# Two gates and two products of the attention's branch behind each retention head, in place of all sixteen tiles behind the last

## The reference

```python
h = rms_norm(x, g_mix[l]); z = h @ w_in[l]
qa, ka, va, ga, ub, vb, qc, kc, vc, gates = split_cols(z)
ya = retention(rotary(qa), rotary(ka), va)          # 4 heads of 128
ya = silu(ga) * rms_normalize(ya) * ret_norm_g[l]
yb = spatial_gating(gelu(ub), gelu(vb), ...)        # 4 groups of 128
yc = dilated window attention(qc, kc, vc)           # 3 groups x 4 heads, mixed by their denominators
gt = sigmoid(gates)                                 # 3 branches x 1024
merged = gt[0] * (ya @ w_branch[l, 0]) + gt[1] * (yb @ w_branch[l, 1]) + gt[2] * (yc @ w_branch[l, 2])
x = x + merged @ w_o[l]
x = x + (silu(rms_norm(x) @ gate) * (rms_norm(x) @ up)) @ w_down[l]
```

## Time and profile before

| what | value |
|---|---|
| median of 3 runs | 1910.8 us (1909.89 to 1911.27) |
| the profiled execution | 1910.71 us |
| its span, first to last instruction | 1908.9 us |
| TensorE, matmuls busy | 1894.6 us, 99% of the span |
| VectorE busy | 1246.4 us, 65% |
| ScalarE busy | 844.4 us, 44% |
| granted TensorE clock over the span | 1.000 |

### The profile page before, as it was taken

How to read it: one execution, slowest core, us unless ns; L and a number is a source line. 1 busy time by engine, 2 the same in 40 slices (tenths; PEclk the granted TensorE clock), 3 DMA queues, 4 the chain that set the end, 5 groups by cost and what they waited for, 6 DMA issues and landing times. The chain is left out here.

```text
span 1908.9 us, 26594 instructions
## 1 busy us (share of the span) xinstructions
PE 1894.6 (99%) x10632; PEld 1699.3 (89%) x10632; DVE 1246.4 (65%) x1625; ACT 844.4 (44%) x1186; POOL 96.9 (5%) x148
## 2 busy tenths in 40 slices
PE   8999999999999999999999999999999999999999
PEld 7888888888888899899888888888888888998998
DVE  7767767746566786377576667677365657863775
ACT  5544444524234464155335444345242344642554
POOL 0000001111111000000000000011111110000000
PEclk9999999999999999999999999999999999999999
DMA  5322356787777355366333222577777773653663
GB/s 203 95 78 67 89 135 182 190 221 206 205 204 207 93 177 173 100 191 198 120 100 95 67 78 83 144 199 185 210 211 211 194 201 92 193 159 107 201 210 122
DMA packets 85897, 295.68 MB, mean 155 GB/s; under 512 B 20368, under 2 KB 20624, under 8 KB 84624
## 3 DMA queue, kind: packets, MB, share of 16 engines
q1 hardware_dynamic: 73104, 218.49, 36.8%
q0 software_dynamic: 12672, 75.51, 17.1%
HBM read 291.79 MB, written 77.66 MB: 194 GB/s over the span
## 5 line engine op out<-in xcount | busy, mean ns | idle before, releaser
L1057 ACT ACTIVATE w_high<-raw 128x1024 fp32r<-128x1024 f32 x396 | 418.3, 1057 | 791.7 <-PE bank L847 663.1
L1266 DVE TENSOR_TENSOR w_low<-raw,w_high 128x1024 fp32r<-128x1024 f32 x396 | 483.0, 1222 | 147.6 <-ACT w_high L1057 141.0
L847 PE MATMUL bank<-h_high,w_high 128*128 128x512 f32 x1408 | 543.5, 386 | 8.9 <-DVE h_low L1271 8.2
L847 PE MATMUL bank<-h_low,w_high 128*128 128x512 f32 x1408 | 534.3, 379 | 0.0
L847 PE MATMUL bank<-h_high,w_low 128*128 128x512 f32 x1408 | 534.1, 379 | 0.0
L847 PEld LDWEIGHTS bank<-h_high,w_high 128*128 128x128 f32 x1408 | 266.7, 189 | 47.0 <-issue 8.1
L847 PEld LDWEIGHTS bank<-h_high,w_low 128*128 128x128 f32 x1408 | 266.6, 189 | 38.0
L847 PEld LDWEIGHTS bank<-h_low,w_high 128*128 128x128 f32 x1408 | 266.8, 189 | 36.2
L847 PE MATMUL bank<-in_high,w_high 128*128 128x512 f32 x672 | 255.0, 379 | 0.0
L847 PE MATMUL bank<-in_low,w_high 128*128 128x512 f32 x672 | 254.7, 379 | 0.0
L847 PE MATMUL bank<-in_high,w_low 128*128 128x512 f32 x672 | 254.7, 379 | 0.0
(11 more groups left out here) (163 smaller groups left out, 2344.3 us busy)
## 6 DMA issues: line engine op xcount, KB each, us to landing
raw<-weights SPq DMA_DIRECT2D x325, 512.0 KB, 4.1
weight_sums<-weights POOLq DMA_DIRECT2D x108, 512.0 KB, 6.1
raw<-weight_sums SPq DMA_DIRECT2D x72, 512.0 KB, 3.8
weight_sums<-weight_sums POOLq DMA_DIRECT2D x36, 512.0 KB, 4.1
turned<-rows SPq DMA_DIRECT2D x3, 768.0 KB, 6.8
xT<-x_t SPq DMA_DIRECT2D x8, 256.0 KB, 5.4
decay_sb<-decay SPq DMA_DIRECT2D x8, 256.0 KB, 5.0
out_t<-xT SPq DMA_DIRECT2D x8, 256.0 KB, 6.4
```

Of the source, the lines that this page charges most:

```text
L847: return pe.matmul(o, w, m, start=start, stop=stop)
L1057: act.activation(w_high[:, PART_SLOT[s], :, :], raw[:, s % RAW_SLOTS, :, :], ACT.Copy).then_inc(part_high_w.sem, 1)
L1266: dve.tensor_tensor(w_low[:, PART_SLOT[s], :, :], raw[:, s % RAW_SLOTS, :, :], w_high[:, PART_SLOT[s], :, :], ALU.subtract).then_inc(part_ ...
```

## The change

The sixteen tiles of `gated(2)` are dealt out: behind the four tiles of retention head h come gate(2, 2h), gate(2, 2h+1), proj(2, 2h), proj(2, 2h+1). The relative places of `schedule` stay as they are, so the steps t+4 to t+7 of every head now hang on these four tiles, and t+8 on rq of the next head, or on sv(0) for head 3. As `merged[7]`, the row that `ret_std` had, is now written before head 3 is through, `ret_std` moves to row 7. As sv(0) now follows the last head directly, the order of the token banks is changed so that `out_bank` comes last, and the wait for the copy out of it stands at the fourth bank's first matmul.

```diff
     for h in range(HEADS):
         t += [("k", h, g) for g in range(N_GROUP)] + [("q", h, g) for g in range(N_GROUP)]
         t += [("v", h, g) for g in range(N_GROUP)]
-    for h in range(HEADS):
-        t += [("rq", h), ("rk", h), ("rv", h), ("rg", h)]
-
-    def gated(branch):
+
+    def gated(branch, pairs=range(KT // 2)):
         out = []
-        for n in range(0, KT, 2):
+        for n in pairs:
+            n *= 2
             out += [("gate", branch, n), ("gate", branch, n + 1), ("proj", branch, n), ("proj", branch, n + 1)]
         return out
 
-    t += gated(2)
+    for h in range(HEADS):
+        t += [("rq", h), ("rk", h), ("rv", h), ("rg", h)] + gated(2, [h])
...
-        ret_std, k_std2 = work[:, 16, :], work[:, 17, :]
+        ret_std, k_std2 = work[:, 7, :], work[:, 17, :]
...
-        token_bank = score_bank + [out_bank, stat_bank]
+        token_bank = score_bank + [stat_bank, out_bank]
...
                 if j == 0:
-                    pe.wait_ge(ret_copied.sem, ret_copied.at(base, HEADS - 1))
                     pe.wait_ge(std_ready.sem, std_ready.at(base, "cq", HEADS - 1))
...
                     for b in range(BLK):
+                        if k == 0 and b == BLK - 1:
+                            pe.wait_ge(ret_copied.sem, ret_copied.at(base, HEADS - 1))
                         hi, lo = (h[:, k, b * P:(b + 1) * P] for h in (h_high, h_low))
```

## The result

| | median us | runs | lowest to highest |
|---|---|---|---|
| before | 1910.59 | 22 | 1909.73 to 1911.59 |
| changed | 1913.12 | 22 | 1912.48 to 1914.03 |

The account below looks back on a forecast made before the run. TensorE was taken as the bound in the retention heads, so only stalls could change: 3.0 - 0.2 = +2.8 us, all other terms 0, giving 1913.5 us; range 1911.0 to 1916.5.

Parts of the forecast that it names:

- (a): Two gates, two projections behind each head: heads 0 to 2 each gain head 3's 0.50 us stall, +3.0 us over two layers.
- (b): Head 3: sv(0) behind its `rowstat` waits for no evacuation, so the last 0.10 us goes: -0.2 us over two layers.
- (c): Token banks reordered, wait for the copy at the fourth bank, `ret_std` in another row: 0, bounds 0 to 0.3 us.
- (d): Seam to the next head: VectorE's rotations, evacuations and splits come right behind the reciprocal; slack 2.0 us, cost 0.
- rival of a backlog: VectorE over 2.0 us later than laid out at the seams; a half-tile slip gives 1917.1 us; chance 0.08.
- (e): Head 0: proj(2,0) reads attention head 3's low half with its tenth matmul; slack 0.42 us, cost 0.
- (f): ScalarE's function tables: 12 loads a layer in place of 10, 5.1 us more of ScalarE, hidden: cost 0.
- (g): Queues of SP and POOL: no DMA added, loads early, POOL's sums keep their place: 0, bounds 0 and 0.5 us.
- rival that interleaving regimes pays: Mixing light tiles between the heads removes TensorE's waits in this stage: faster, 1909.1 us; chance 0.05.

Follow-up runs that it names:

- early_rpv: Changed kernel with `rpv`, copy and squares one tile earlier in heads 1 to 3, and the squares' subtraction behind the first projection's evacuation in all heads: 1909.92 us.
- evac_first: Changed kernel with VectorE's subtraction (low half of the squares) moved behind the first projection's evacuation: 1912.70 us.
- after_twice_inv: Changed kernel with the reciprocal of each head's deviation done twice, 3.4 us more VectorE work a head: 1928.77 us.
- no_sigmoid: Changed kernel with Silu in place of Sigmoid in the eight gates of branch 2, table loads down from 22 to 14: 1913.79 us.
- early_all: early_rpv with head 0's `rowstat` and reciprocal one tile later and its rowscale four tiles behind that: 1909.66 us.
- before_early3: Kernel before, with head 3's `rpv`, copy and squares one tile earlier and its subtraction behind the evacuation: 1909.26 us.
- late_rowstat: Changed kernel with `rowstat`, reciprocal and what follows one tile later in all heads: 1926.83 us.
- before_late3: Kernel before, with `rowstat` of head 3 alone and what follows it one tile later: 1914.44 us.

## Why the prediction was right, step by step

(a) Held in place, mechanism and size: 0.50 us a head, in heads 0 to 2 of both layers, the stall of head 3 in the earlier trace rows again. early_rpv shows that it is the cover, evac_first splits it into 0.40 and 0.10.

(b) Held: behind head 3 only 0.32 + 0.08 us remain. (a) and (b) make 1.40 us a layer; the stage grew by 1.40. The sum of +2.8 us stands against 2.5 measured, interval 1.3 to 3.8.

(c) Held: no wait at sv(0); behind its `rowstat` sv(0) starts on time in the changed kernel (420.19 to 420.40). No run changes the banks or the row of `ret_std` alone, but (a) and (b) leave nothing of the stage's 1.40 us for them.

(d) Right in its result, 0 us, and wrong in its slack. I laid out VectorE's queue correctly (rv out at 390.7 in head 3's times, 18.8 us behind the start of the tile after `rowstat`; in head 1's it was out at 354.64 + 0.68 = 355.32, 18.8 behind 336.51), but held only its last item against TensorE's need. The item before it, the bank of rk, has the nearer deadline: 1.3 us of slack. The rival of a backlog would have decided at 1.3 us, and I had given it its chance by 2.0; that the cost was 0 all the same owes something to luck. The wrong slack cost the expectation of after_twice_inv 0.7 us a seam.

(e) Held to 0.01 us: in the changed kernel the last attention head's low half is ready at 287.22 + 0.69 = 287.91 and the tenth matmul of proj(2,0) starts at 288.34: 0.43 us to spare, 0.42 forecast. VectorE and TensorE, answering to the earlier trace rows:

```profile
287.22 0.69 DVE L1467 TENSOR_TENSOR in_low<-bank,in_high 128x512 fp32r<-128x512 f32 x1 [5.46 <-ACT in_high L1205]
```
```profile
288.34 0.38 PE L847 MATMUL bank<-in_high,w_high 128*128 128x512 f32 x1
```

(f) Held: 22 table loads in front of the activations of tiles in place of 18, hidden, as no_sigmoid shows by taking eight of them away for nothing. The Trainium skill's rule to batch functions by set (ScalarE: Activation LUTs, Table sets: the hidden batching unit) is no guide in this stage, where TensorE is the bound and ScalarE had been idle for 3.10 us when the chain of head 1 reached it; here it would have named a wrong cause.

(g) Held so far as the traces show: no new wait of TensorE for a weight, and 20.78 us of POOL in the stage against 21.59.

The rival that interleaving regimes pays is refuted for this stage by early_all against before_early3. It was the busy share of VectorE (71% in the heads in the earlier trace rows; 66% over the whole stage before, 62% over the dealt one) that could have suggested it; but TensorE had waited for nothing in the heads.

What I had not seen, and what the misses of late_rowstat and before_late3 taught, is that the stall of the earlier trace rows had two bounds on one another. I had written that the evacuation adds 0.10 us; without the `rowstat` in front the wait is worth 0.93. My sum needed only the pair as it stood, and so came out right.

## What to carry to other kernels

A chain across engines is covered by the length of the tile that stands beside it, so a reorder that puts a half tile where a full one stood can cost time though the engine that is the bound has not one instruction more; look for a place in the trace where the new neighbourhood already exists, and read the price there. Before a waiting step is moved later, ask what waits behind it for the same queue: its own work may be the cover of the next wait. And hold every item of a laid-out queue against its own deadline, not the last item alone.

## What the hardware showed beyond that

In after_twice_inv the first layer's stage is 181.58 us, 1.68 longer than the second's. TensorE stood still for 2.0 us, from 310.50, when its next matmul was due, to 312.54, as it did at each of six seams; but behind this one alone the granted clock fell, about 0.8 us after it had resumed. TensorE in order of time, then five stretches of 2 us; the clock is the number behind the POOL column:

```profile
310.29 0.38 PE L847 MATMUL bank<-h_high,w_low 128*128 128x512 f32 x1
312.54 0.48 PE L847 MATMUL bank<-h_high,w_high 128*128 128x512 f32 x1 [1.87 <-DVE scaled L1376]
...
313.32 0.63 PE L847 MATMUL bank<-h_high,w_high 128*128 128x512 f32 x1
```
```profile
310.00:312.00 2.00, 0.67 (x4) 0.23 (x2) 1.95 (x4) 1.06 (x1) 0.00 (x0) 1.00 0.51 205
312.00:314.00 2.00, 1.46 (x5) 1.26 (x6) 2.00 (x3) 0.00 (x0) 0.68 (x2) 0.81 0.00 0
314.00:316.00 2.00, 2.00 (x6) 1.55 (x6) 1.94 (x4) 0.00 (x0) 1.02 (x2) 0.50 0.68 152
316.00:318.00 2.00, 2.00 (x10) 1.69 (x8) 2.00 (x3) 0.00 (x0) 0.00 (x0) 0.84 1.04 262
318.00:320.00 2.00, 2.00 (x13) 1.76 (x12) 0.07 (x1) 0.23 (x1) 0.00 (x0) 1.00 1.06 207
```

From 313.32 to 316.31 the matmuls stood 0.43 us apart in place of 0.215, the lower of the two levels (1.2 in place of 2.4 GHz). A stall of 2.0 us thus cost 3.7 once in six times. The other three executions of after_twice_inv have mean granted clocks of 0.999, 0.999 and 0.998, where all 22 of the changed kernel have 1.000, so it is likely to have fallen there too. The six stalls of 1.95 us of late_rowstat left it at full level in the profiled execution, as did the stalls of 0.3 us of this change. Why it fell at one seam and not at the others stays open.
